# Summing the modulation rows over the partitions: from TensorE products with ones to DRAM transposes and GpSimd adds

## The chip, the cores and the metric

One core of a Trainium2 chip (trn2) runs the program once. The metric is the device time of that one execution in microseconds (us), lower is better. Times are given as the median of several runs of one build; the profile comes from one execution of its own.

## The reference, cut to what matters

The program computes two transformer-like blocks on 256 tokens of width 2048: a first block (a gated recurrence, dilated attention, output product) and a second block of two layers whose normalised inputs are modulated. Only the modulation is touched by the change:

```python
s_lat = jax.nn.silu(c)              # (1, 2048)
s_ctx = jax.nn.silu(c_ctx)          # (2048,)
for l in range(DEPTH_2):            # two layers
    shift, scale, gate = jnp.split((s_lat @ w_mod[l] + b_mod[l])[:, None, :], 3, axis=-1)
    shift_c, scale_c, gate_c = jnp.split(s_ctx @ w_mod[l] + b_mod[l], 3, axis=-1)
    hx = _rmsnorm(x, norm_g[l]) * (1.0 + scale) + shift
    hc = _rmsnorm(ctx, norm_g[l]) * (1.0 + scale_c) + shift_c
    ...
        ctx = ctx + gate_c * y_c
    x = x + gate * y
```

`w_mod[l]` is 2048 x 6144 in float32. A vector times this matrix is wanted for two vectors (one for the last gate).

## The kernel before

**The main work.** All large products run in *granules*: 256 rows of a weight matrix by 512 columns. ScalarE (ACT) writes the high half `w_hi` of the weights (line 607), VectorE (DVE) the low half `w_lo` (line 615), and TensorE (PE) does twelve products of 128x512 with them (lines 626, 627, 632). ACT and DVE may be up to four granules ahead (`NSPLIT = 4`). SyncE (SP) loads the weights into a ring of four slots (`raw`), each for two granules, in the order of the list `LOADS`. A granule `n` also carries side work, written out by hand at fixed numbers: attention, recurrence, normalisation. The stages are the first part (granules 0 to 223, four iterations of 56), the branches (`S2` on), the output product (`S3` on), and four streams of the second block, `c0`, `x0`, `c1`, `x1` (from `S4` on).

**The modulation.** `w_mod` is worked off in twelve *halves* (`HALVES`): a layer, a part (shift, scale or gate) and 1024 of its columns, for two vectors, or for one in halves 10 and 11. For each half, DVE multiplies 16 tiles of 128 rows by the vector's value of that row and adds them up into `rows` (128 partitions x 1024) for each vector, one operation at a time, at the granules that the table `HALVES` gives (`mod_row`, lines 2246 and 2250). What is left is the sum of `rows` over the 128 partitions.

Before, this sum is made by TensorE, in `mod_half` at the granules of the table `SUMS`: products with a column of ones into rows 0, 32, 64 and 96 of the PSUM tile `X[3]`.

```python
for j in range(2):
    for v in range(values):
        r = 32 * (values * j + v)
        last = pe.matmul(X[3][r:r + 1, :], ones, rows[h][v][:, CH * j:CH * (j + 1)], start=True, stop=True)
last.then_inc(mod_sums, 1)
```

Four granules later DVE copies the sums out of PSUM (`chunk_copy`, line 2259) or adds the gate's bias (`gate_add`, line 2267). GpSimd (POOL) sends shift and scale through DRAM (`col_mid`, line 794) so that they come back as columns over the partitions (`modcol`, line 797), to which DVE adds the bias (`columns_read`, line 2277); a gate goes to DRAM (`m_mid`, line 786), and is read from there over all partitions when a stream ends.

**Who else waits.** `mod_sums` also tells that the memory of `rows` is free. SP waits for it before two loads of the modulation's own slots (`load_own`, lines 546 and 561), ACT before it writes `o_hi`, `u_hi`, `m_hi`, `stg2` and `b_hi`, DVE before `u_lo` and before halves 4 and 7, and POOL before it loads half of the context `xr_p3` (line 924). This context is squared by ACT at granule `S3 + 13` (line 1500). POOL's program is a fixed order of its own: the first six halves, the two gates of layer 0, the loads around `S3`, then `windows`, `pairs` and `ends` of each stream. `windows` is a run of GpSimd adds and products (lines 856 to 867); `pairs(s)` gives the low half of two keys `kq_lo` (line 883) for each of four pairs of heads, which TensorE's scores (line 1302) take; in the first part `rope` on DVE (lines 2125 to 2132) turns queries and keys that TensorE then transposes (`t_qk`, line 961).

Of the kernel before, what the change touches and what calls it, by code (L numbers as in the profile page):

```python
# [15 lines left out]
F32 = mybir.dt.float32  # L16
F32R = mybir.dt.float32r
ALU = mybir.AluOpType
# [135 lines left out]
COLUMNS_BEFORE = [sum(not g for g in IS_GATE[:e]) for e in range(len(SUMS) + 1)]  # L154
GATES_BEFORE = [sum(IS_GATE[:e]) for e in range(len(SUMS) + 1)]
GATE_EVENTS = [e for e in range(len(SUMS)) if IS_GATE[e]]
LAYER_COLUMNS = [1 + max(COLUMNS_BEFORE[e] for e in range(len(SUMS)) if not IS_GATE[e] and HALVES[e].layer == l) for l in range(LAYERS)]

# [5 lines left out]
OPS_AT = [[(h, t, i) for g, h, t, i in OPS if g == n] for n in range(GRANULES)]  # L164

# [82 lines left out]
def build_program(nc, t, out):  # L248
    with ExitStack() as ctx:
# [63 lines left out]
        modchunk2 = at("modchunk2", rt + 36 * KB, [P, CH])  # L313
# [28 lines left out]
        gaterows = [at(f"gaterows{i}", a, [P, CH]) for i, a in enumerate((cm + 2048, cm + 2048, regU + 28 * KB, regH + 14 * KB))]  # L342
# [9 lines left out]
        ones = small[:, 40:41]  # L352
# [69 lines left out]
        col_mid = nc.dram_tensor("col_mid", (COLUMNS_BEFORE[-1], 2, HALF), F32, kind="Internal").ap()  # L422

# [46 lines left out]
        mod_chunk, mod_cols, mod_read = sem("mod_chunk"), sem("mod_cols"), sem("mod_read")  # L470
        mod_rows, mod_sums, rows_in = sem("mod_rows"), sem("mod_sums"), [sem(f"rows_in{i}") for i in range(2)]
# [60 lines left out]
        def load_own(sp, item):  # L532
# [8 lines left out]
            elif h == 9 and i == 4:  # L541

                sp.wait_ge(*ST[0].at("gpT_ps", 1))
                sp.wait_ge(*ST[0].at("win", 12))
            elif h == 7 and i == 3:
                sp.wait_ge(mod_sums, 7)
# [13 lines left out]
            elif h == 6:  # L560
                sp.wait_ge(mod_sums, 6)
# [75 lines left out]

        def chunk_of(e):

            return modchunk2 if e == 9 else modchunk  # L640
# [122 lines left out]
        def _(pool):  # L763

            pool.memset(modchunk[:, :], 0.0).then_inc(mod_zero, 1)
            pool.memset(ones, 1.0).then_inc(mod_zero, 1)
# [6 lines left out]
            def gate_bias(l, i, half, values):  # L773
                pool.memset(gaterows[i][:, :], 0.0).then_inc(mod_zero, 1)
                pool.wait_ge(mod_zero, 3 + i + 1)
                for j in range(2):
                    for v in range(values):
                        r, col = 32 * (values * j + v), HALF * half + CH * j
# [2126 lines left out]
```

## Time and profile before

| | |
|---|---|
| median of 3 runs | 2459.67 us (2459.33 to 2459.93) |
| the profiled execution's own time | 2459.43 us |
| its span in the trace | 2457.6 us |
| TensorE matmul busy | 2444.9 us, 99% |
| VectorE busy | 2079.3 us, 85% |
| ScalarE busy | 1279.9 us, 52% |
| GpSimd busy | 132.7 us, 5% |
| granted TensorE clock | 0.999 of full |
| DMA | 570.35 MB, 232 GB/s on the mean |

The span is what the trace covers; the execution's own time is 1.83 us longer. A busy TensorE means that matmul records follow each other without a gap; their ends are modelled, so the distance between two starts tells more than a record's length. In the rows, PE is TensorE's matmuls, DVE VectorE, ACT ScalarE, POOL GpSimd; "out<-in" names tiles by the program's names, and "idle before <-releaser" is how long the engine had nothing before the row, and what ended it.

### The profile page before, as it was taken

The page shows a single profiled execution, that of the slowest core. Times are in us where ns is not written, and L with a number is a line of the kernel's source. Part 1 is how long each engine was busy: PE and PEld are TensorE (multiplying, and loading weights), DVE is VectorE, ACT ScalarE, POOL GpSimd, SP SyncE. Part 2 cuts the span into 40 slices and gives each one's busy share as a digit, 9 for nine tenths or more (in the row PEclk, how much of TensorE's full clock was granted, in tenths as well). Part 3 has the DMA queues.
Part 4 walks back from the last instruction along what each step waited for, and adds up shares of the span by engine and source line. Part 5 has one row for each costly group of instructions (what it writes and reads, how often), then busy time and mean ns, then how long its engine had stood idle before and what let it go on. Part 6 is the DMA issues. An engine that isn't in the chain of part 4 may idle for free.

```text
span 2457.6 us, 30476 instructions
## 1 busy us (share of the span) xinstructions
PE 2444.9 (99%) x11640; PEld 2010.3 (82%) x11640; DVE 2079.3 (85%) x2655; ACT 1279.9 (52%) x1761; POOL 132.7 (5%) x196
## 2 busy tenths in 40 slices
PE   9999999999999999999999999999999999999998
PEld 7888888888788888888888888888888888888887
DVE  6999898898988998768999877898977885988876
ACT  6545544544554344454455654455565444456664
POOL 0000000000000000100200000110000000200000
PEclk9999999999999999999999999999999999999999
DMA  9877687586769787778655577754547876554464
GB/s 356 271 247 254 206 282 238 188 281 228 251 212 326 259 304 269 279 249 287 205 189 187 180 265 280 283 172 155 171 154 257 286 280 218 176 166 150 148 225 152
DMA packets 351905, 570.35 MB, mean 232 GB/s; under 512 B 19376, under 2 KB 204080, under 8 KB 347920
## 3 DMA queue, kind: packets, MB, share of 16 engines
q1 hardware_dynamic: 343232, 532.87, 63.7%
q0 software_dynamic: 7808, 34.79, 4.2%
q8 instruction: 92, 1.51, 0.3%
q10 hardware_dynamic: 720, 0.75, 0.1%
q14 instruction: 53, 0.43, 0.0%
HBM read 559.85 MB, written 8.48 MB: 231 GB/s over the span
## 4 chain that ended last, share of the span: by engine, by line
PE 97%; DVE 1%; issue 1%; ACT 0%; DMA 0%; SPq 0%; DVEq 0%
PE acc L626 30%; PE acc L627 29%; PE acc L632 29%; PE aux L961 3%; PE aux L1328 2%; PE aux L1302 1%; PE aux L1104 0%; PE aux L994 0%; DVE w_lo L615 0%; PE aux L1297 0%; DVE rows_u L2250 0%; PE aux L1051 0%; DMA raw<-in_w_in 0%; PE aux L1445 0%; PE aux L1443 0%
## 5 line engine op out<-in xcount | busy, mean ns | idle before, releaser
L607 ACT ACTIVATE w_hi<-raw 128x1024 fp32r<-128x1024 f32 x808 | 846.0, 1059 | 759.1 <-PE acc L632 643.0
L615 DVE TENSOR_TENSOR w_lo<-raw,w_hi 128x1024 fp32r<-128x1024 f32 x808 | 990.8, 1230 | 253.7 <-ACT w_hi L607 252.3
L626 PE MATMUL acc<-w_hi,h_hi 128*128 128x512 f32 x2240 | 885.6, 395 | 1.6 <-ACT w_hi L607 1.6
L627 PE MATMUL acc<-w_hi,h_lo 128*128 128x512 f32 x2240 | 873.1, 390 | 0.0
L632 PE MATMUL acc<-w_lo,h_hi 128*128 128x512 f32 x2240 | 600.6, 390 | 0.0
L626 PEld LDWEIGHTS acc<-w_hi,h_hi 128*128 128x128 f32 x2240 | 420.5, 188 | 96.5 <-issue 6.9
L632 PEld LDWEIGHTS acc<-w_lo,h_hi 128*128 128x128 f32 x2240 | 420.3, 188 | 89.5 <-DVE w_lo L615 0.7
L627 PEld LDWEIGHTS acc<-w_hi,h_lo 128*128 128x128 f32 x2240 | 420.7, 188 | 84.7
L626 PE MATMUL acc<-w_hi,u_hi 128*128 128x512 f32 x800 | 316.5, 396 | 0.0
L627 PE MATMUL acc<-w_hi,u_lo 128*128 128x512 f32 x800 | 312.0, 390 | 0.0
L632 PE MATMUL acc<-w_lo,u_hi 128*128 128x512 f32 x800 | 214.3, 390 | 0.0
L2599 DVE SCALAR_TENSOR_TENSOR cacc<-upad,wdw,cacc 128x256 f32<-128x256 f32 x360 | 192.6, 535 | 5.5
L626 PEld LDWEIGHTS acc<-w_hi,u_hi 128*128 128x128 f32 x800 | 150.2, 188 | 34.2 <-ACT w_hi L607 2.3
L632 PEld LDWEIGHTS acc<-w_lo,u_hi 128*128 128x128 f32 x800 | 150.2, 188 | 31.9
L627 PEld LDWEIGHTS acc<-w_hi,u_lo 128*128 128x128 f32 x800 | 150.2, 188 | 29.9
L2250 DVE SCALAR_TENSOR_TENSOR rows_u<-rows_in,smod,rows_u 128x1024 f32<-128x1024 f32 x75 | 97.8, 1311 | 0.1
L1798 ACT ACTIVATE prb<-aux,sm 128x512 f32<-128x512 f32 (+1 forms) x96 | 57.9, 616 | 37.8 <-DVE sm L2529 37.1
L2527 DVE TENSOR_REDUCE sm<-aux 128x1 f32<-128x512 f32 (+1 forms) x96 | 51.0, 595 | 3.7 <-PE aux L1302 3.6
L626 PE MATMUL acc<-w_hi,m_hi 128*128 128x512 f32 x128 | 50.7, 396 | 0.0
L627 PE MATMUL acc<-w_hi,m_lo 128*128 128x512 f32 x128 | 50.0, 390 | 0.0
L1806 ACT ACTIVATE aT<-aux 128x512 f32<-128x512 f32 (+1 forms) x48 | 22.6, 525 | 48.6 <-PE aux L1328 33.7
L794 POOL DMA_DIRECT2D col_mid<-modchunk x16 | 9.1, 568 | 717.9 <-DVE modchunk L2259 717.9
(389 smaller groups left out, 2165.7 us busy)
## 6 DMA issues: line engine op xcount, KB each, us to landing
raw<-in_w_in SPq DMA_DIRECT2D x630, 512.0 KB, 4.7
rows_in<-in_w_mod SPq DMA_DIRECT2D x120, 512.0 KB, 6.2
raw<-in_w_out SPq DMA_DIRECT2D x96, 512.0 KB, 4.8
raw<-in_w_mod SPq DMA_DIRECT2D x72, 512.0 KB, 5.7
raw<-in_w_rnn_out SPq DMA_DIRECT2D x32, 512.0 KB, 6.4
raw<-in_w_o SPq DMA_DIRECT2D x32, 512.0 KB, 8.0
raw<-in_w_attn_out SPq DMA_DIRECT2D x16, 512.0 KB, 4.9
xr_s<-x_mid POOLq DMA_DIRECT2D x4, 1024.0 KB, 12.2
```

Of the source, the lines that this page charges most:

```text
L607: act.activation(w_hi[:, n % NSPLIT], raw[:, slot, (n % 2) * SK:(n % 2) * SK + SK], ACT.Copy).then_inc(hi_ready, 1)
L615: dve.tensor_tensor(w_lo[:, n % NSPLIT], raw[:, slot, (n % 2) * SK:(n % 2) * SK + SK], w_hi[:, n % NSPLIT].bitcast(F32), ALU.subtract).the ...
L626: pe.matmul(acc[pair][m][:, :], a_hi[:, k0 + k, token(m)], w_hi[:, s, k], start=start and k == 0, stop=False)
L627: pe.matmul(acc[pair][m][:, :], a_lo[:, k0 + k, token(m)], w_hi[:, s, k], start=False, stop=False)
L632: last = pe.matmul(acc[pair][m][:, :], a_hi[:, k0 + k, token(m)], w_lo[:, s, k], start=False, stop=stop and k == SK - 1)
L961: return pe.transpose(dst.bitcast(F32R), src, ident[:, :])
L1302: last = pe.matmul(X[2 * comp + m][:, :], q_part[r, tokens], k_part[r, T:3 * T], start=i == 0, stop=i == 2)
L1328: last = pe.matmul(X[3][:, (2 * h + m) * P:(2 * h + m + 1) * P], aT[:, 4 * m + k], v, start=k == 0, stop=k == nk - 1)
L1798: act.activation(prb[:, b, 0:nk * P], X[b][:, 0:nk * P], ACT.Exp, bias=sm[:, 12 + b:13 + b], scale=SCALE2, accum_out=sm[:, 16 + b:17 + b]) ...
L2250: i = dve.scalar_tensor_tensor(out=dst, in0=src, scalar=smod[:, k, v:v + 1], in1=dst, op0=ALU.mult, op1=ALU.add)
L2527: step.link(dve.tensor_reduce(sm[:, 8 + b:9 + b], X[b][:, 0:nk * P], AX.X, ALU.max, negate=True))
L2599: i = dve.scalar_tensor_tensor(out=dst, in0=src, scalar=w, in1=dst, op0=ALU.mult, op1=ALU.add)
```

## The change

TensorE's products with ones, their copies out of PSUM and the semaphore `mod_sums` go. Each half is now summed by POOL alone. `rows_out` writes `rows` to DRAM (`row_mid`) in blocks of 128 columns. `fold` reads it back so that a partition holds 4 x 128 values of one column block, adds quarter on quarter, then halves; what is left (128 x 128) goes to DRAM again (`part_mid`) and is folded the same way on 16 (or 8) partitions. Then the bias is added and the result goes where it went before. Whoever waited for `mod_sums` now waits for `rows_gone`, the landing of the writes.

```diff
-SUMS = [(h, TAIL_SG[0] + 15 if h == 9 else AT[h][-1] + 2) for h in range(len(HALVES))]
+FOLDS = [[at(f"fold{i}{j}", off, [P, 4, P]) for j, off in enumerate(pair)] for i, pair in enumerate((
+    (regU + 12 * KB, regU + 14 * KB), (regO + 6 * KB, regO + 14 * KB), (cm + 2048, o3 + 28 * KB),
+    (rt + 6 * KB, rt + 101 * KB // 2)))]
+def rows_out(e):
+    pool.wait_ge(mod_rows, OPS_BEFORE[e + 1])
+    for v in range(HALVES[e].values):
+        pool.dma_start(row_mid[e][8 * v:8 * v + 8].rearrange("k p c -> p k c"),
+                       rows[e][v][:, :].rearrange("p (k c) -> p k c", k=8)).then_inc(rows_gone, 16)
+def fold(e, place):
+    x = HALVES[e]
+    a, b = FOLDS[place]
+    blocks = 8 * x.values
+    groups = P // blocks
...
+    def down(src, parts, count):
+        brought(pool.dma_start(a[0:parts], src[:, 0:4]))
+        for q in range(4, count, 4):
+            brought(pool.dma_start(b[0:parts], src[:, q:q + 4]))
+            pool.wait_ge(folding, folded)
+            added(pool.tensor_tensor(a[0:parts], a[0:parts], b[0:parts], ALU.add))
+        added(pool.tensor_tensor(a[0:parts, 0:2], a[0:parts, 0:2], a[0:parts, 2:4], ALU.add))
+        added(pool.tensor_tensor(a[0:parts, 0:1], a[0:parts, 0:1], a[0:parts, 1:2], ALU.add))
+    pool.wait_ge(rows_gone, GONE[e + 1])
+    down(row_mid[e][0:blocks].rearrange("k (g r) c -> (k g) r c", g=groups), P, P // groups)
+    brought(pool.dma_start(part_mid[e], a[:, 0]))
+    pool.wait_ge(folding, folded)
+    down(part_mid[e].rearrange("(k g) c -> k g c", g=groups), blocks, groups)
...
-for e in range(6):
-    move_columns(e)
+for e in range(3):
+    rows_out(e)
+    fold(e, 0)
+for e in (3, 4):
+    rows_out(e)
+    fold(e, 1)
+rows_out(5)
 pool.wait_ge(oT_lo, IT1)
...
+fold(5, 2)
+for e in (6, 7):
+    rows_out(e)
+    fold(e, 2)
...
                     for h in range(2):
                         pool.tensor_tensor(kq_lo[h][:, 2 * T:], kc[:, 2 * p + h, :], kq_hi[h][:, 2 * T:].bitcast(F32),
                                            ALU.subtract).then_inc(S["keys_r"], 1)
+                    if p < 2:
+                        fold((8, 9)[p] if s == 1 else (10, 11)[p], 3)
...
-            pool.wait_ge(mod_sums, 9)
+            rows_out(8)
+            pool.wait_ge(rows_gone, GONE[9])
             pool.dma_start(xr_p3[:, 0], t["ctx_2"][0][0:P, :]).then_inc(ST[0]["xr_in"], 16)
...
                         if it:

-                            act.wait_ge(mod_sums, U_FREE[it])
+                            act.wait_ge(rows_gone, GONE[U_FREE[it]])
```

Beside this, `windows` of `x0` and `x1` issues `rows_out(10)` and `rows_out(11)`, and `ends` of `c0` issues `rows_out(9)`. The last lines of the diff are one of the waits (ACT before `u_hi`); the others are changed in the same way, and half 4 on DVE and the last part of `o_hi` on ACT now wait for earlier folds to be done (`mod_read`).

The order of instructions shows three places. **TensorE at the end of the first iteration**, before (the sums of half 0):

```order
L632 MATMUL acc<-w_lo,h_hi 128x512 [waits lo_ready]
L632 MATMUL acc<-w_lo,h_hi 128x512 x3
L1104 MATMUL aux<-rows_u_117,small 1x512 [waits mod_rows]
L1104 MATMUL aux<-rows_u_118,small 1x512
L1104 MATMUL aux<-rows_u_117,small 1x512
L1104 MATMUL aux<-rows_u_118,small 1x512
L626 MATMUL acc<-w_hi,h_hi 128x512 [waits hi_ready,ev1_dve,ev1_act]
```

The four middle rows are gone, here and at the eleven other places (two rows for halves 10 and 11).

**POOL in stream x0**, between the key pieces of two pairs of heads, in the changed kernel; before, the third row here followed the second at once:

```order
L922 TENSOR_TENSOR kq_lo_186<-kc,kq_hi_184 128x256
L800 DMA fold_118<-row_mid 128x512 [waits rows_gone]
L802 DMA fold_119<-row_mid 128x512
L804 TENSOR_TENSOR fold_118<-fold_118,fold_119 128x512 [waits folding]
...
L806 TENSOR_TENSOR fold_118<-fold_118 16x128 [waits fold_step]
L826 DMA col_mid<-fold_118 16x128 [waits fold_step]
L831 DMA modcol_90<-col_mid 128x8x1 [waits folding]
L836 TENSOR_TENSOR modcol_90<-modcol_90,modbias 128x16 [waits folding]
L922 TENSOR_TENSOR kq_lo_185<-kc,kq_hi_183 128x256 [waits s_sc_ps,s_qkT_sb]
```

A whole fold (eight adds, one bias add, and ten loads and stores) now stands in front of the next pair's keys.

**POOL around the context load of `S3`**, before:

```order
L922 DMA xr_p_208<-in_ctx 128x2048 [waits m_lo_r,gate_out]
L924 DMA xr_p_208<-in_ctx 128x2048 [waits mod_sums]
L794 DMA col_mid<-modchunk 2x512 [waits mod_chunk]
```

and in the changed kernel:

```order
L960 DMA xr_p_211<-in_ctx 128x2048 [waits m_lo_r,gate_out]
L775 DMA row_mid<-rows_z_134 128x8x128 [waits mod_rows]
L775 DMA row_mid<-rows_z_135 128x8x128
L963 DMA xr_p_211<-in_ctx 128x2048 [waits rows_gone]
L860 DMA wdw<-in_columns 128x124
```

The second context load now waits for the landing of two stores that are issued behind the first one.

## Rows read from the trace of the kernel before

**Rows 1.** The page, chain that ended last: shares of the span.
```profile
PE 97%; DVE 1%; issue 1%; ACT 0%; DMA 0%; SPq 0%; DVEq 0%
```
**Rows 2.** Timeline of PE: start us, us, engine line op out<-in xcount.
```profile
169.49 1.07 PE L632 MATMUL acc<-w_lo,h_hi 128*128 128x512 f32 x4
170.48 1.04 PE L1104 MATMUL aux<-rows_u,small 128*1 128x512 f32 x8
...
171.79 0.39 PE L627 MATMUL acc<-w_hi,h_lo 128*128 128x512 f32 x1
...
173.41 1.07 PE L632 MATMUL acc<-w_lo,h_hi 128*128 128x512 f32 x4
...
174.54 0.39 PE L627 MATMUL acc<-w_hi,h_lo 128*128 128x512 f32 x1
```
**Rows 3.** Timeline of PE around the sums of half 11, of one vector.
```profile
2034.40 1.07 PE L632 MATMUL acc<-w_lo,u_hi 128*128 128x512 f32 x4
...
2036.69 0.39 PE L627 MATMUL acc<-w_hi,u_lo 128*128 128x512 f32 x1
```
**Rows 4.** Groups of POOL by shape: busy us, mean ns of one, idle before.
```profile
L858 POOL TENSOR_TENSOR win_a<-win_b 128x562 f32<-128x562 f32 x3 | 3.6, 1193 | 0.2
L864 POOL TENSOR_TENSOR win_b<-win_b,rcnt 128x256 f32<-128x256 f32 x6 | 5.6, 938 | 0.5
```
**Rows 5.** Timeline of DVE as POOL's adds of stream x0 begin.
```profile
1588.46 0.99 DVE L2599 SCALAR_TENSOR_TENSOR cacc<-upad,wdw,cacc 128x256 f32<-128x256 f32 x2
...
1590.52 4.08 DVE L2599 SCALAR_TENSOR_TENSOR cacc<-upad,wdw,cacc 128x256 f32<-128x256 f32 x2
1594.52 2.15 DVE L615 TENSOR_TENSOR w_lo<-raw,w_hi 128x1024 fp32r<-128x1024 f32 x1
```
**Rows 6.** Windows: us, PE PEld DVE ACT POOL busy, PEclk, DMA share, GB/s.
```profile
740.00:780.00 40.00, 40.00 (x193) 32.52 (x192) 35.66 (x36) 14.84 (x17) 5.62 (x10) 1.00 0.92 340
1590.00:1607.00 17.00, 17.00 (x77) 14.06 (x76) 16.86 (x14) 7.67 (x9) 15.44 (x14) 1.00 0.38 123
1640.00:1750.00 110.00, 110.00 (x566) 90.30 (x564) 97.89 (x164) 62.23 (x111) 4.31 (x6) 1.00 0.50 163
```
**Rows 7.** Tile view of `col_mid`: DMA issues to landing.
```profile
DMA to landing us min/median/max: 2.1/5.3/12.8
```
**Rows 8.** Timeline of DVE, two places.
```profile
326.65 0.28 DVE L2132 TENSOR_TENSOR qk<-qk,rtmp 128x128 f32<-128x128 f32 x1
...
772.13 1.23 DVE L615 TENSOR_TENSOR w_lo<-raw,w_hi 128x1024 fp32r<-128x1024 f32 x1
```
**Rows 9.** Timeline of PE, four places.
```profile
327.07 0.79 PE L961 MATMUL aux<-ident,qk_r 128*128 128x128 f32 x8
...
671.42 0.80 PE L961 MATMUL aux<-ident,qk_r 128*128 128x128 f32 x7 [1.22 <-DVE qk L2132]
...
774.54 1.07 PE L632 MATMUL acc<-w_lo,h_hi 128*128 128x512 f32 x4
...
1045.90 0.39 PE L626 MATMUL acc<-w_hi,m_hi 128*128 128x512 f32 x1
```
**Rows 10.** Groups of DVE by shape: what copies the sums out.
```profile
L2259 DVE COPY modchunk<-aux 128x512 f32<-128x512 f32 x8 | 5.5, 685 | 0.0
```
**Rows 11.** Timeline of POOL around `S3`.
```profile
1023.91 0.54 POOL L922 DMA_DIRECT2D xr_p<-in_ctx  x1 [82.97 <-DVE m_lo L2422]
1027.12 0.54 POOL L924 DMA_DIRECT2D xr_p<-in_ctx  x1 [2.67 <-PE aux L1104]
```
**Rows 12.** The page, DMA issues: xcount, KB each, median us to landing.
```profile
xr_p<-in_ctx POOLq DMA_DIRECT2D x2, 1024.0 KB, 8.5
```
**Rows 13.** Timeline of ACT at granules `S3 + 13` and `S3 + 14`.
```profile
1037.75 1.90 ACT L1500 ACTIVATE squares_out<-xr_p 128x2048 f32<-128x2048 f32 x1
...
1039.64 1.05 ACT L607 ACTIVATE w_hi<-raw 128x1024 fp32r<-128x1024 f32 x1
```
**Rows 14.** Waits of POOL: us in total, times, longest us.
```profile
POOL kq_lo L883 <- ACT kq_hi L1791: 311.3, 6, 51.9
```

More of the change, by code:

```diff
@@ L147 @@
 assert all(len(x.at) == 2 * x.values * HALF_TILES and x.at == sorted(x.at) for x in HALVES)
-SUMS = [(h, TAIL_SG[0] + 15 if h == 9 else AT[h][-1] + 2) for h in range(len(HALVES))]
 IS_GATE = [x.part == 2 for x in HALVES]
[L154 to L157, printed above, removed]
+COLUMNS_BEFORE = [sum(not g for g in IS_GATE[:e]) for e in range(len(HALVES) + 1)]
+GATES_OUT = [16 * sum(HALVES[i].values for i in range(e + 1) if IS_GATE[i]) for e in range(len(HALVES))]
+LAYER_COLUMNS = [1 + max(COLUMNS_BEFORE[e] for e in range(len(HALVES)) if not IS_GATE[e] and HALVES[e].layer == l) for l in range(LAYERS)]
 OPS_BEFORE = [0]
@@ L164 @@
 OPS_AT = [[(h, t, i) for g, h, t, i in OPS if g == n] for n in range(GRANULES)]
+GONE = [0]
+for x in HALVES:
+    GONE.append(GONE[-1] + 16 * x.values)
 def rows_after(h, t):
@@ L769, in _ @@
             pool.tensor_copy(ident[:, :], ident_in[:, :]).then_inc(const_in, 1)
[L773 to L778, printed above, removed]
-                        pool.dma_start(gaterows[i][r:r + 1, :], t["b_mod_2"][l:l + 1, 2 * D + col:2 * D + col + CH]).then_inc(tables_in, 16)
@@ L781, in gate_rows @@
-            def gate_rows(l, i, half, values):
-                pool.wait_ge(mod_chunk, GATE_EVENTS[i] + 1)
-                for j in range(2):
-                    for v in range(values):
-                        r, col = 32 * (values * j + v), HALF * half + CH * j
-                        pool.dma_start(m_mid[l, v:v + 1, col:col + CH], gaterows[i][r:r + 1, :]).then_inc(gate_out, 16)
-            def move_columns(e):
-                c = COLUMNS_BEFORE[e]
-                l, first = HALVES[e].layer, HALVES[e].part * KT + 8 * HALVES[e].half
-                pool.wait_ge(mod_chunk, e + 1)
-                for j in range(2):
-                    pool.dma_start(col_mid[c][:, CH * j:CH * (j + 1)], chunk_of(e)[64 * j:64 * j + 33:32, :]).then_inc(mod_cols, 16)
-                pool.wait_ge(mod_cols, 64 * c + 32)
-                for v in range(2):
-                    pool.dma_start(modcol[l][:, first:first + 8, v], col_mid[c][v].rearrange("(k p) -> p k", p=P),
-                                   allow_slow_non_contiguous=True).then_inc(mod_cols, 16)
@@ L1704, in sides @@
                         if chunk:
-                            act.wait_ge(mod_sums, (0, 6, 8, 8)[chunk])
+                            act.wait_ge(rows_gone, GONE[(0, 6, 8, 8)[chunk]])
                             if chunk != 2:
```

160 lines of the change are left out of this document (60 added, 100 removed).

## The prediction

> **What bounds the kernel now.** I began with the chain of waits that ended last: 97% of the span is TensorE [rows 1], and the product lines 626, 627 and 632 hold nearly all of it. So whatever leaves TensorE's queue shortens the run by its full spacing, as long as its helpers keep their lead: ACT and DVE prepare each granule, and TensorE stalls only where that preparation comes late. I then read the timelines of PE, DVE, ACT and POOL side by side, to see how far ahead the preparation is, and looked for the few places where it is nearly late. The question of this change is how much of a sure gain on TensorE is given back there. The clock plays no part: the windows show it at 1.00, the upper level of 2.4 GHz, and TensorE has no pause in which that would change [rows 6].
>
> **What is removed.** From the first `w_lo` product of a granule to the second product of the next one takes 174.54 - 173.41 = 1.13 us; with the sums between them 171.79 - 169.49 = 2.30 us [rows 2]. One half costs 1.17 us. The sums of half 11, of one vector and half as many products, take just as much: 2036.69 - 2034.40 = 2.29 us [rows 3], so the number of products does not count here. Twelve halves: 12 x 1.17 = **14.0 us off TensorE**. They all lie on the chain, so they count in full. DVE loses twelve copies or adds of about 0.69 us [rows 10] and eight small bias adds; POOL loses its few memsets and its small DMAs. None of these is on the chain.
>
> **What is added on POOL.** A half costs two stores of 512 KB (one for halves 10 and 11), then a fold: seven transfers one after the other (three quarters of `row_mid`, the first two loads side by side; `part_mid` out; `part_mid` in; `col_mid` or the bias; `modcol` or `m_mid`), and nine adds. A POOL add takes 1.19 us for 562 elements and 0.94 for 256 [rows 4]. So four adds of 512 at about 1.12, two of 256 at 0.8 to 0.9, two of 128 at about 0.6 and a small bias add make some 7.6 us. A transfer: those of `col_mid` land after 5.3 us in the median, 2.1 at best and 12.8 at worst [rows 7]. A fold is thus 7 x 5.3 + 7.6 = about 45 us, with 22 and 97 as the bounds if every transfer were the best or the worst. Two halves are about 100 us apart, so POOL itself has time. What this does to others is the point.
>
> **DVE beside POOL's adds.** While POOL is busy 15.4 of 17 us [rows 6], DVE's operations stretch: a pair of taps from 0.99 to 4.08 us, `w_lo` from 1.23 to 2.15 [rows 5]. These two pieces are the first of eight in that stretch; the six after them lose 0.5 to 0.9 us each, and all eight 8.1 us: about 0.5 us of DVE for each us of POOL. The bounds are none (DVE was waiting anyway) and 1. Where DVE's lead is several us this is covered. In the first part it is not covered everywhere: the transposes of rotated queries and keys start at 327.07, and DVE's last piece for them ends at 326.65 + 0.28 = 326.93; those at 671.42 even waited 1.22 us for DVE [rows 8, 9]. There DVE is one granule ahead, not four. Half 1 ends at about 269 and its fold runs from about 278 to 325; half 4 ends at 622.5 and its fold runs from about 632 to 680. DVE works without a gap from about 309 to 327 and from about 651 to 671. Into the first stretch fall the small adds of the fold's second half, some 2.5 us: 1.3 us of DVE, less the 0.14 of slack and a little that DVE no longer does: +1.0. Into the second fall one add of 512, the two small ones, and the three of the second half, 5 us: +2.4. Sum **+3.4 us**, bounds 0 and 7.
>
> **SBUF ports.** In the stretch above, POOL's adds cost DVE about half their time. The Trainium skill (SBUF — State Buffer, Who interferes with whom) speaks against this change: a DVE instruction with two SBUF inputs and a GpSimd instruction that reads SBUF use one shared interface, and the one that comes second blocks for the whole of the other. By that rule each us of POOL would cost DVE up to a full us; the first pair of taps looks like it, the stretch as a whole does not.
>
> **DMA near 770 us.** From 740 to 780 us the DMA engines are busy 0.92 of the time at 340 GB/s [rows 6], and this is where the weights arrive last: `w_lo` is ready at 772.13 + 1.23 = 773.36, and TensorE takes it at 774.54 [rows 8, 9], a lead of 1.18 us. The first loads of fold 5 fall here, together 1 MB: at 340 GB/s 3.1 us of transfer more, and 1 us of adds beside DVE, less the copy of 0.6 to 0.7 at this place that goes [rows 10]: late by 3.4, stall **+2.2 us**. If the loads spread over a longer time it is 0; if SP also waits for the stores of half 5 before its own loads behind them, 6.
>
> **The context at `S3`.** Before, the two context loads are issued at 1023.91 and 1027.12 and land after 8.5 us each, the second at 1035.6 [rows 11, 12]. ACT squares it at 1037.75, and the next `w_hi`, ready at 1039.64 + 1.05 = 1040.7, is wanted by TensorE at 1045.90 [rows 13, 9]. So the second load may come 2.1 + 5.2 = 7.3 us later without a stall. In the change, two stores are issued behind the first load, at about 1024.5, and take the place of the second load: they land at about 1035.8. Then the second load is issued and needs its 8.5 us: 1044.3, late by 8.7, stall **+1.4 us**. Bounds: 0 if it lands in 6 us or so, 6 if the stores take 5 us longer.
>
> **Other waits** I take at nothing. `u_hi` and `u_lo` of iterations 1 to 3 come more than 10 us after the stores of the half before have landed; `m_hi` of the third branch chunk comes 17 us after half 7's last row; halves 9 to 11 leave behind waits that stood there before. If the cover were gone each would cost ACT a few us. The DMA engines carry 2 x 10 + 1 x 2 = 22 MB more on 570, mostly where they have room.
>
> **Sum**, against the profiled execution: 2459.43 - 14.0 + 3.4 + 2.2 + 1.4 = 2452.4. The median stands 0.24 above that execution: **2452.7 us**. About 0.2% (4.9 us) is what a measurement of this kernel can tell from no change; 7.0 us is over it.
>
> **The rivals.** *All is covered.* If DVE's losses fall into its idle time and the transfers into gaps, only the 14.0 us remain: 2445.7. For it: DVE is busy 85% on the whole. Against it: the three places above, where the lead is 0.1, 1.2 and 7 us.
>
> *Full blocking.* If each us of POOL costs DVE a full us, the places cost 2.3, 4.9 and (3.1 + 2 - 0.6 - 1.2) = 3.3, with the context's 1.4 together 11.9: 2457.6, no change. The first pair of taps, 3.1 us lost in 4, speaks for it; 8.1 lost in 15.4 over the whole stretch, against it. It is the rule of the SBUF page named above.
>
> *The folds hold up the keys (slower).* In streams `x0` and `x1` folds 8 to 11 stand between the key pieces of two pairs of heads. POOL waited 51.9 us there for ACT [rows 14]; with the 1.7 us until TensorE's scores begin a fold may last 53.6. At 45 us it fits. But all seven transfers are in series, and one that is late moves TensorE, which has nothing else to do then. Each of four folds costs its excess: with folds of 60 us 4 x 6.4 = 25.6, so 2478.3; it outweighs the gain of 7.0 from 55.4 us on. For it: the landing times up to 12.8. Against it: from 1640 to 1750 us the DMA engines are busy only 0.50 at 163 GB/s [rows 6], while the median of 5.3 comes mostly from busier stretches. The Trainium skill (DMA: Bandwidth & Descriptors, Anatomy of one DMA) gives about 2.0 us fixed and bytes at 436 GB/s for a transfer; by that a fold is an estimated 24 us and this rival falls away.
>
> *Late stores.* If a store of a half takes 15 us and more, SP, ACT at `u_hi` and the context all wait: 5 to 10 us more each, 2460 to 2475.
>
> **How the numbers follow.** My forecast's mechanism (2449.5 to 2456.5) 0.45, all covered 0.22, full blocking 0.19, the keys 0.09, late stores 0.05. Below 2454.8 lie the second, and most of the first: faster 0.59. Within 0.2%, up to 2464.6: the rest of the first, full blocking, half of late stores: 0.29. Slower 0.12. The range leaves out some of the bottom, where 2445.7 is nearly a floor, and the keys: 2446.0 to 2463.5; the bounds of the three stalls together (0 and 19, less 14.0) would reach from 2445.7 to 2464.7.
>
> **What would show it.** In the changed profile granules without side work should follow each other at 2.72 us at the former twelve places, with no L1104. POOL's busy time should grow by about 90 us to 220. Rows of DVE beside POOL's adds should be longer by half of these. PE should wait at the transposes near 320 and 660 for DVE, and stand near 765 and near 1035 on `w_hi` or `w_lo`. A fold should last about 45 us from its first load to its last, and the key pieces in `x0` and `x1` should still wait for ACT. I am wrong in my main step if TensorE's gaps sum to less than 3 or more than 11 us; if `kq_lo` is released by a fold, the keys' rival has it; if TensorE stands on `squares_out` for over 5 us, the stores were priced too low.

## The result and the profile after

The changed kernel takes **2486.88 us** (median of 4 runs, 2486.24 to 2487.21), the kernel before 2459.57 us (2459.33 to 2459.93) beside it: ratio 1.011, 95% interval 1.0097 to 1.0122. It is 27.3 us slower; the forecast was 7.0 us faster, with a range up to 2463.5. The profiled execution took 2487.15 us, with a span of 2485.3.

The page of the changed kernel, with what answers to the table of before and to [rows 1]: busy times (us, share, instructions), then the chain that ended last.

```profile
PE 2445.2 (98%) x11552; PEld 2015.3 (81%) x11552; DVE 2122.4 (85%) x2635; ACT 1275.9 (51%) x1761; POOL 344.8 (14%) x385
...
PE 72%; DVE 14%; DMA 5%; issue 5%; ACT 3%; SPq 0%; POOL 0%; DVEq 0%; ACTq 0%; POOLq 0%
```

TensorE held 97% of the chain before; now DVE, the DMA queues and ACT stand in it with 22%. POOL grew by 212 us (forecast: 90): 158 of them are the adds of the folds, the rest is mostly the issuing of transfers, which the page counts as busy. DVE grew by 43 although it lost twelve copies.

The saving itself is there. The timeline of PE where the first sums were, which answers to [rows 2]:

```profile
172.34 1.07 PE L635 MATMUL acc<-w_lo,h_hi 128*128 128x512 f32 x4
...
175.06 1.07 PE L635 MATMUL acc<-w_lo,h_hi 128*128 128x512 f32 x4
```

2.72 us from granule to granule, where 3.92 stood. Set side by side product by product, the two timelines of PE show this step of 1.1 to 1.2 us at eleven of the twelve places. At the twelfth (half 9, 1431 us before) only 0.4 us are gained, because a wait of 0.47 us for `w_hi` takes the sums' place. So 13.3 us left TensorE, for the 14.0 of the forecast. What ate them, the waits of PE (us in total, times, longest):

```profile
PE aux L995 <- DVE qk L2133: 10.1, 5, 4.9
PE acc L629 <- ACT w_hi L610: 8.2, 6, 4.8
PE aux L995 <- DVE og L2155: 7.7, 2, 4.7
PE acc L635 <- DVE w_lo L618: 1.8, 4, 0.7
PE aux L995 <- DVE prb L2504: 1.7, 1, 1.7
PE aux L1150 <- POOL rx L765: 1.3, 1, 1.3
PE aux L1309 <- DVE u_lo L2528: 0.6, 1, 0.6
PE aux L1085 <- DVE xc L2176: 0.3, 1, 0.3
```

That is 31.7 us, against 4.5 in the kernel before (qk 1.6, `w_hi` 1.6, `rx` 1.3). 27.2 of waits do not make up 27.7 + 13.3 = 41.0. The next part is the clock. The windows of 8 us right behind four of the waits (columns as in [rows 6]):

```profile
568.98:576.98 8.00, 8.00 (x34) 6.69 (x35) 8.00 (x8) 3.26 (x5) 2.05 (x3) 0.79 0.68 205
686.79:694.79 8.00, 8.00 (x29) 6.62 (x30) 6.53 (x6) 2.88 (x4) 0.90 (x1) 0.65 0.76 257
1069.00:1077.00 8.00, 8.00 (x24) 6.40 (x25) 5.36 (x8) 7.23 (x8) 0.00 (x0) 0.65 0.88 283
2258.12:2266.12 8.00, 8.00 (x36) 6.65 (x36) 7.93 (x10) 4.53 (x6) 5.18 (x5) 0.79 0.42 134
```

PE is busy all of the time, with a granted clock of 0.65 to 0.79 on the mean: part of each window ran at the lower level of 1.2 GHz (from 686 to 692 us the windows show 0.50 throughout). 8 x (0.21 + 0.35 + 0.35 + 0.21) = 9.0 us lost behind the waits, not in them. In the timeline a product stands 0.43 us from the next there and not 0.23. So 36 of the 41 us have a name; the rest is in steps too small for a row of their own. The kernel before shows 1.00 in the 8 us behind its longest inner wait, 1.22 us at 671.42 [rows 9].

By place, from the two timelines of PE (waits with the clock behind them, at times of the kernel before): fold 0 at 218 us 3.0; fold 1 at 307 and 328 4.1; fold 3 at 561 6.4; fold 4 from 650 to 675 9.0; fold 5 near 780 some 2; the context at 1046 7.8; fold 11 at 2233 4.0; small steps elsewhere together some 5. These are the places where a fold runs beside; how much of each the fold itself causes is taken apart behind the experiments.

What the adds of a fold took (POOL by shape: busy us, mean ns of one, idle before):

```profile
L804 POOL TENSOR_TENSOR fold<-fold,fold 128x512 f32<-128x512 f32 x32 | 58.5, 1828 | 156.2 <-DMA fold<-row_mid 156.2
L804 POOL TENSOR_TENSOR fold<-fold,fold 16x512 f32<-16x512 f32 x10 | 20.7, 2066 | 42.8 <-DMA fold<-part_mid 42.8
...
L806 POOL TENSOR_TENSOR fold<-fold 16x128 f32<-16x128 f32 x10 | 11.8, 1181 | 0.8
```

1.83 us for 512 elements on the mean (forecast 1.12), and a small add on 16 partitions costs as much as one on 128: 2.07 us for 512 elements and 1.18 for 128 (forecast for the last: about 0.6). These means hold the waits for DVE. The adds that met none took 1.28, 0.80 and 0.53 us for 512, 256 and 128 elements, on 128 partitions and on 16, close to the forecast. A fold took 48 to 60 us from its first load to its last add in the first eight, 43 in `x0` and 29 in `x1`, for the forecast's 45.

### The profile page after: what moved, and what is told of

It reads as the page before. It is cut to its first block, busy times and chain, and to the rows that moved or that the text cites. A ratio compares the mean times of both kernels' runs of the same rounds, so it can differ in the third digit from the quotient of the medians.

```text
span 2485.3 us, 30445 instructions
## 1 busy us (share of the span) xinstructions
PE 2445.2 (98%) x11552; PEld 2015.3 (81%) x11552; DVE 2122.4 (85%) x2635; ACT 1275.9 (51%) x1761; POOL 344.8 (14%) x385
## 4 chain that ended last, share of the span: by engine, by line
PE 72%; DVE 14%; DMA 5%; issue 5%; ACT 3%; SPq 0%; POOL 0%; DVEq 0%; ACTq 0%; POOLq 0%
PE acc L629 22%; PE acc L630 22%; PE acc L635 22%; DVE w_lo L618 5%; DMA raw<-in_w_in 3%; PE aux L995 2%; ACT w_hi L610 1%; PE aux L1335 1%; DVE rows_m L2251 1%; DVE rows_u L2251 1%; PE aux L1309 1%; DVE rows_o L2251 1%; DMA rows_in<-in_w_mod 1%; DMA raw<-in_w_mod 1%; DVE cacc L2561 0%
## 5 line engine op out<-in xcount | busy, mean ns | idle before, releaser
L618 DVE TENSOR_TENSOR w_lo<-raw,w_hi 128x1024 fp32r<-128x1024 f32 x808 | 1001.4, 1244 | 250.8 <-ACT w_hi L610 249.2
L2561 DVE SCALAR_TENSOR_TENSOR cacc<-upad,wdw,cacc 128x256 f32<-128x256 f32 x360 | 201.2, 559 | 5.5
L804 POOL TENSOR_TENSOR fold<-fold,fold 128x512 f32<-128x512 f32 (+2 forms) x48 | 89.3, 1861 | 210.8 <-DMA fold<-row_mid 156.2
```

The lines of the kernel that those rows point to most:

```text
L618: dve.tensor_tensor(w_lo[:, n % NSPLIT], raw[:, slot, (n % 2) * SK:(n % 2) * SK + SK], w_hi[:, n % NSPLIT].bitcast(F32), ALU.subtract).the ...
L804: added(pool.tensor_tensor(a[0:parts], a[0:parts], b[0:parts], ALU.add))
L2561: i = dve.scalar_tensor_tensor(out=dst, in0=src, scalar=w, in1=dst, op0=ALU.mult, op1=ALU.add)
```

## The experiments

The theory to start from: POOL's adds slow DVE, DVE's lead is thin in the first part, and TensorE waits. The rival: the folds' loads and stores do it. Thirteen kernels answer; times are medians of 4 to 10 runs, which lie within 0.3 to 5.5 us of each other, each group beside its own runs of the kernel before (2459.42 to 2459.62).

**1. The adds left out.** In `down`:

```diff
-                        added(pool.tensor_tensor(a[0:parts], a[0:parts], b[0:parts], ALU.add))
-                    added(pool.tensor_tensor(a[0:parts, 0:2], a[0:parts, 0:2], a[0:parts, 2:4], ALU.add))
-                    added(pool.tensor_tensor(a[0:parts, 0:1], a[0:parts, 0:1], a[0:parts, 1:2], ALU.add))
+                    pool.wait_ge(folding, folded)
```

> All nine of POOL's adds inside a fold are left out but the last bias add of shift and scale, so the modulation is not summed; every store, load and wait of POOL stays. In the changed kernel's trace TensorE loses about 41 us in stalls against the 14 it gains: some 33 at places beside a fold, 7.6 at the context. Theory A (the adds slow DVE, which has little lead there): these 33 go, the context stays: 2486.9 - 32 = about 2455, between 2452 and 2458. Theory B (the folds' loads and stores delay the weights): no more than 5 us of it goes: 2482 to 2487. Theory C (half and half): near 2470.

(The gate's bias add stays as well: the eight adds of `down` are what is left out.)

Measured: 2463.99 us (ratio 1.0017, 1.0008 to 1.0026), between theory A's range and theory C. The adds cost 22.9 us and are the largest part, but not the 32 that theory A gave them.

**2. The folds' loads left out as well.** Both `down` calls and the store of partial sums are replaced by one memset.

```diff
-                down(row_mid[e][0:blocks].rearrange("k (g r) c -> (k g) r c", g=groups), P, P // groups)
-                brought(pool.dma_start(part_mid[e], a[:, 0]))
-                pool.wait_ge(folding, folded)
-                down(part_mid[e].rearrange("(k g) c -> k g c", g=groups), blocks, groups)
+                added(pool.memset(a[0:blocks, 0:1], 0.5))
```

> The fold's loads, its store of partial sums, their loads and all adds are left out too (the modulation is not summed); a memset of 16 values takes their place. The stores of rows to DRAM and everything that waits for them stay, and so do the last small transfers. Theory A: as without adds, within 1.5 us: 2453 to 2456. Theory B: this is where the time goes, 2452 to 2455 and at least 20 us under the kernel without adds. The context's 7.6 us stay in both.

Measured: 2457.07 us, above both ranges. The folds' loads, without any adds, cost 6.9 us; both theories had this wrong, A by calling it nothing.

**3. Tiny stores.**

```diff
-                    pool.dma_start(row_mid[e][8 * v:8 * v + 8].rearrange("k p c -> p k c"),
-                                   rows[e][v][:, :].rearrange("p (k c) -> p k c", k=8)).then_inc(rows_gone, 16)
+                    pool.dma_start(row_mid[e][8 * v, 0:1, :], rows[e][v][0:1, 0:P]).then_inc(rows_gone, 16)
```

> As the kernel without folds, but each store of rows is one partition's 512 bytes, so the stores' bytes go too, while the order of waits stays (the modulation is not summed). Both theories: the context's stall falls from 7.6 us to under 2, and about 2446 to 2449 remains, which is the kernel before less 12 x 1.17. If it stays at 2453 the context's stall is not the stores' length but the order of POOL's queue.

Measured: 2451.5 us (ratio 0.9966, 0.9955 to 0.9978). The context's stall went from 5.6 to 0.4 us, so it was the stores' length. But the time is above the expected range, and 6 us above the 2445.4 that TensorE's queue alone would give, with next to nothing left of the change. Two waits for DVE remain: 1.1 us at 557 and 3.45 at 669, with the clock at 0.79 in the 8 us behind that one. The windows view of this kernel:

```profile
640.00:680.00 40.00, 36.55 (x166) 29.96 (x165) 37.00 (x42) 15.07 (x18) 0.00 (x0) 0.96 0.63 212
```

DVE is busy 37.0 of 40 us, and POOL not at all. By 632 us TensorE had gained 5 x 1.1 us, DVE had not, and here they meet. (That DVE's load is the cause is an argument up to here; experiment 9 tests it.)

**4. The order at the context.**

```diff
+            rows_out(8)
             pool.wait_ge(m_lo_r, 2 * NCH)
             pool.dma_start(xr_p3[:, 1], t["ctx_2"][0][P:2 * P, :]).then_inc(ST[0]["xr_in"], 16)
-            rows_out(8)
             pool.wait_ge(rows_gone, GONE[9])
```

> Only the order at the context: the two stores of half 8 are issued before POOL waits for the last low half of the third branch, ahead of the first context load instead of behind it. Half 8 is ready about 5 us before that wait ends. If the 7.6 us there are the stores' landing, they shrink to under 2: 2486.9 - 6 = about 2481, between 2479 and 2483. If the stall has another origin (the DMA engines are full, and the load itself is late), under 2 us go: 2485 to 2487.

The place in the changed kernel, POOL and then PE, which answers to [rows 9, 11]:

```profile
1044.35 0.57 POOL L960 DMA_DIRECT2D xr_p<-in_ctx  x1 [42.14 <-DVE m_lo L2384]
1044.90 1.83 POOL L775 DMA_DIRECT2D row_mid<-rows_z  x2
1057.27 0.56 POOL L963 DMA_DIRECT2D xr_p<-in_ctx  x1 [10.53 <-DMA row_mid<-rows_z]
```
```profile
1069.00 0.80 PE L629 MATMUL acc<-w_hi,m_hi 128*128 128x512 f32 x1 [4.84 <-ACT w_hi L610]
```

Measured: 2486.74 us (2485.23 to 2490.47): no change that can be told from none, as the second case has it. The edit did what it should: the second context load is issued 7.4 us behind the first and no longer 12.9. But TensorE then waits in two places (timeline of PE, this kernel):

```profile
1054.94 0.50 PE L629 MATMUL acc<-w_hi,m_hi 128*128 128x512 f32 x1 [2.07 <-ACT w_hi L610]
...
1068.93 0.50 PE L629 MATMUL acc<-w_hi,m_hi 128*128 128x512 f32 x1 [2.55 <-ACT w_hi L610]
```

Before the first of them ACT waited 5.85 us for `raw<-in_w_o`, before the second 4.42, while its square no longer waits for the context (7.03 us in the changed kernel). So the late transfer is now one of the weights and not the context. That the stores and the context's loads, now closer together, delay the weights is the likely reading; no run here tests it by itself.

**5. The adds made twice.** Each of the three lines of experiment 1 stands twice in a row.

> Each of a fold's adds but the bias adds is made twice (the modulation's values are changed by it), with the same loads, stores and waits. In the changed kernel the adds keep POOL busy 158 us and, against the kernel without them, cost 22.9 us of time. Theory A (POOL and DVE slow each other while both work): the second helping costs at least as much as the first, since the cover is used up: 2486.9 + 23 to 45 = 2510 to 2532, with more and longer waits of TensorE for DVE. Theory B (a fold that ends later holds up those who wait for it): TensorE, ACT or DVE would be released by POOL, and 13 us more per fold would cost nothing where a fold ends 50 us early: 2487 to 2495.

Measured: 2533.2 us (ratio 1.0299), 46.3 us more, a little over the range of theory A. The second helping costs twice the first. Theory B is out: no wait of TensorE names a fold; those for DVE (`qk`, `prb`, `og`, `w_lo`, `xc`) rose from 21.6 to 49.2 us.

**6. Only the adds on 128 partitions.**

```diff
-                        added(pool.tensor_tensor(a[0:parts], a[0:parts], b[0:parts], ALU.add))
+                        if parts == P:
+                            added(pool.tensor_tensor(a[0:parts], a[0:parts], b[0:parts], ALU.add))
+                    if parts < P:
+                        pool.wait_ge(folding, folded)
+                        return
```

> Of the adds only the five on 128 partitions stay in each fold (for two vectors); the adds on 16 or 8 partitions are left out, so the modulation is not summed. The small ones are about a third of POOL's add time (some 50 of 158 us). Theory A1 (what counts is how long POOL works, however few partitions): a third of the 22.9 us goes: 2476 to 2481. Theory A2 (an add on 16 partitions hardly disturbs DVE): 2485 to 2488.

Measured: 2475.24 us (2473.27 to 2476.65), 0.8 below A1's range and far from A2's. Half of the 22.9 us belongs to the adds on 16 or 8 partitions, which do some 6% of the arithmetic of the others (896 x 16 beside 1920 x 128 elements). They are 60 of the 148 us of the adds left out in experiment 1, 40% and not the third that was expected. A2 is out: few partitions are no cheaper.

**7. Half 5's work moved behind the transposes, with tiny stores and no folds**, by the table of halves.

```diff
     Half(1, 0, 1, 2, None, tiles_at((3 * SG1, (
-        45, 46, 46, 47, 48, 48, 49, 50, 53, 53, 54, 55)), (S2, (
-        0, 0, 1, 4, 5, 5, 6, 7, 10, 10, 11, 12, 13, 17, 17, 18, 18, 19, 19, 20)))),
+        52, 52, 53, 53, 54, 54, 55, 55)), (S2, (
+        0, 0, 1, 2, 3, 4, 5, 5, 6, 7, 8, 9, 10, 11, 12, 13, 14, 15, 16, 17, 18, 19, 19, 20)))),
```

> The kernel with tiny stores and no folds (the modulation is not summed; 2451.5 us, with 3.45 us of TensorE waiting for DVE at the transposes near 669 us and a lower clock behind it), and the multiply-adds of half 5 that stood in the seven granules ahead of that place are moved behind it by the table of halves, with the same work in all. Theory (DVE sets the pace there, so TensorE's gain of the four halves before is lost at it): the wait goes and the clock stays up: 2451.5 - 5 = about 2446.5, between 2445 and 2448. Rival (the weights come late, DVE only passes it on): 2450 to 2452.

Measured: 2455.22 us, worse by 3.7 and outside both ranges. The wait at 669 is gone (5.1 us less there, with the clock), but 7.1 us came back behind it, with waits of 1.26 us at 717 and this one, in the timeline of PE:

```profile
733.27 0.94 PE L991 MATMUL aux<-ident,s_sb_r 128*128 128x128 f32 x9 [3.29 <-DVE og L2151]
```

From 680 to 735 us DVE is now busy 48.3 of 55 us and was 45.3 in experiment 3's kernel: the room behind the transposes is as small as the room ahead of them.

**8. The same move in the changed kernel.**

> The changed kernel with the same move of half 5's multiply-adds and nothing else. Theory: the 9.0 us that TensorE loses around 672 us go, with a part coming back at the transposes after it because fold 4 still runs: 2478 to 2482. Rival (DVE is behind everywhere there and the loss only moves): 2484 to 2488.

Measured: 2488.65 us, 0.65 above the rival's range, and the rival's case: in the timelines of PE 8.2 us go between 640 and 700 us, and 9.4 come between 700 and 760.

**9. Less work for DVE, with tiny stores and no folds.** It tests the same theory as 7 without moving work to another place where DVE has no room.

```diff
                 dst = rows[h][v][:, :].rearrange("p (a c) -> p a c", a=2)
+                if 3 <= h <= 5 and (tile or j):
+                    src, dst = src[:, 0:1, :], dst[:, 0:1, :]
```

> The kernel with tiny stores and no folds (the modulation is not summed; 2451.5 us), and in halves 3 to 5 each of DVE's multiply-adds but the first of a half works on 512 of its 1024 columns (0.7 in place of 1.3 us), with the same loads. Theory (DVE's own load is what keeps TensorE from taking its whole gain between 540 and 780 us): no wait for DVE is left there, also not the 1.22 us of the kernel before: 2451.5 - 5.3 = about 2446, between 2445 and 2448. Rival (weights that land late, whatever DVE does): 2450 to 2453.

Measured: 2445.57 us (ratio 0.9944, 0.9929 to 0.9959). With room on DVE TensorE takes its whole gain. The window that answers to experiment 3's:

```profile
640.00:680.00 40.00, 40.00 (x192) 33.39 (x191) 32.44 (x42) 17.04 (x19) 0.00 (x0) 1.00 0.79 274
```

DVE 32.4 in place of 37.0 us, TensorE without a gap, and 0.79 of the DMA engines' time in place of 0.63: the weights were not what was late. Beside experiment 3's kernel 1.3 us are gained at 557 and 5.3 around 669, and nothing over 0.3 elsewhere.

**10. The same in the changed kernel.**

> The changed kernel, whole folds, with the same smaller multiply-adds in halves 3 to 5 (part of the modulation is not computed). TensorE loses 16 us there between 560 and 680 us. Theory (a fold costs only what DVE's lead does not cover): under 4 us of it stay and the rest of the run is as it was: 2471 to 2477. Rival (a fold costs TensorE the same whether DVE has time or not): 2483 to 2487.

Measured: 2472.17 us (2469.30 to 2473.95), 14.7 less. Of the 16 us between 560 and 680 a wait of 2.3 stays (in the profiled execution, the fastest of the four). A fold costs what DVE cannot cover.

**11. The folds' adds without the loads between them.** `down` loses its loads and their waits, and `a` and `b` are set to zero first.

> The folds' adds in full, on zeros, without the folds' loads and without the store of partial sums (the modulation is not summed); the stores of rows stay. Without its loads a fold's adds follow each other at once, some 13 us in one piece. The kernel without loads and adds takes 2457.1 us, loads without adds cost 6.9, loads and adds 29.8. Theory (adds and loads cost apart): 2457.1 + 22.9 = 2480, between 2475 and 2485. Rival (the adds hurt because they come in single pieces over 50 us and wait for DMA in between): under 2470, if one compact stretch fits into DVE's lead.

Measured: 2488.72 us, 31.7 above the kernel without folds and outside both ranges: one compact piece is no better, and adds and loads do not add up. The adds cost 31.7 us without the loads and 22.9 beside them; adds and loads together cost 29.8. So the split between them depends on the order in which they are taken away. (The 24 memsets that this kernel adds are free, by experiment 13.) This kernel also shows how an add acts. POOL, then DVE in this kernel, then DVE at the same place in the kernel of experiment 9, where POOL is idle:

```profile
173.75 4.16 POOL L801 TENSOR_TENSOR fold<-fold,fold 128x512 f32<-128x512 f32 x3
```
```profile
172.97 0.74 DVE L2166 TENSOR_SCALAR qk<-acc,small 128x512 f32<-128x512 f32 x1
173.85 1.47 DVE L2123 TENSOR_TENSOR rtmp<-qk,rope 128x256 f32<-128x256 f32 x1
175.36 1.40 DVE L2125 TENSOR_TENSOR qk<-qk,rope 128x256 f32<-128x256 f32 x1
176.86 1.20 DVE L2129 TENSOR_TENSOR qk<-qk,rtmp 128x128 f32<-128x128 f32 x1
```
```profile
173.87 0.42 DVE L2122 TENSOR_TENSOR rtmp<-qk,rope 128x256 f32<-128x256 f32 x1
174.33 0.42 DVE L2124 TENSOR_TENSOR qk<-qk,rope 128x256 f32<-128x256 f32 x1
174.86 0.29 DVE L2128 TENSOR_TENSOR qk<-qk,rtmp 128x128 f32<-128x128 f32 x1
```

Three adds of 1.39 us, and three DVE operations of 0.42, 0.42 and 0.29 us that each last about as long as an add: DVE lost 2.9 us in 4.2. `L2166`, ahead of them, stands beside a memset of POOL and keeps its time. It also works the other way. Two adds of the changed kernel (POOL, then DVE, fold 0):

```profile
187.36 4.14 POOL L804 TENSOR_TENSOR fold<-fold,fold 128x512 f32<-128x512 f32 x1 [5.38 <-DMA fold<-row_mid]
...
198.34 1.29 POOL L804 TENSOR_TENSOR fold<-fold,fold 128x512 f32<-128x512 f32 x1 [5.99 <-DMA fold<-row_mid]
```
```profile
186.80 1.27 DVE L2251 SCALAR_TENSOR_TENSOR rows_b<-rows_in,smod,rows_b 128x1024 f32<-128x1024 f32 x1
188.00 2.34 DVE L618 TENSOR_TENSOR w_lo<-raw,w_hi 128x1024 fp32r<-128x1024 f32 x2
190.27 1.00 DVE L2138 SCALAR_TENSOR_TENSOR s_sb<-aux,mask 128x384 f32<-128x384 f32 x2
...
198.46 2.25 DVE L618 TENSOR_TENSOR w_lo<-raw,w_hi 128x1024 fp32r<-128x1024 f32 x1 [2.09 <-ACT w_hi L610]
```

The first add begins while DVE works. The three operations with two inputs in SBUF keep their times, and the add ends 1.16 us after the last of them: POOL paid 2.9 us, DVE nothing. The second begins 0.12 us ahead of `w_lo`. It keeps its time, and `w_lo` takes 2.25 us in place of 1.22: DVE pays. So who pays is settled by who comes first, and a us of POOL's adds cost DVE less than a us on the mean. Not every operation of DVE takes part. These two rows of the changed kernel (DVE, then POOL) overlap, and both have the times that they have alone:

```profile
1694.11 2.48 DVE L2489 TENSOR_REDUCE sm<-aux 128x1 f32<-128x512 f32 x4 [0.24 <-PE aux L1309]
```
```profile
1695.90 1.28 POOL L804 TENSOR_TENSOR fold<-fold,fold 16x512 f32<-16x512 f32 x1 [4.12 <-DMA fold<-part_mid]
```

`aux` is in PSUM; DVE's other operations with an input in PSUM keep their times beside adds as well.

**12. Copies in place of adds.**

```diff
-                        added(pool.tensor_tensor(a[0:parts], a[0:parts], b[0:parts], ALU.add))
+                        added(pool.tensor_copy(a[0:parts], b[0:parts]))
```

(and the two lines after it in the same way)

> Each add of a fold but the bias adds becomes a POOL copy of the same shape, one input in place of two (the modulation is not summed); loads, stores and waits stay. Theory A (DVE loses while POOL reads SBUF, in proportion to POOL's time): the cost over the kernel without adds falls with POOL's busy time; copies of about half the adds' duration would give 2464.0 + 11 = 2475, between 2468 and 2481. Theory B (it is the number of instructions, each holding up one DVE operation for good, whatever its length): 2484 to 2488. Theory C (only two-input instructions of POOL disturb DVE): 2462 to 2466.

Measured: 2468.71 us, 4.7 over the kernel without adds. It lies at the lower end of A's range, but A's proportion does not hold: the copies keep POOL busy for 94 us and the adds for 148, which would give 14.6. B is out, since there are as many instructions. C nearly fits: a copy costs something, but far less than an add.

**13. Memsets in place of adds**, `pool.memset(a[0:parts], 0.0)` and so on.

> As the copies, with memsets of the same shape: POOL only writes (the modulation is not summed). A memset of 128x512 took 0.53 us in the kernel with adds alone. Theory A1 (it is POOL's reading that DVE waits for): nothing but the loads and stores is left, 2462 to 2466, and DVE's small operations beside the memsets keep their 0.4 and 0.3 us. Theory A2 (any use of SBUF by POOL counts, in proportion to its time): 100 memsets of 0.5 us are a third of the adds' time: about 2464 + 7 = 2471, between 2468 and 2474.

Measured: 2462.89 us, as without adds (2463.99): A1. 38 of DVE's `w_lo` lie beside a memset and take 1.22 us, the time that they take alone; 60 lie beside a fold's add in the changed kernel and take 1.45 on the mean, up to 2.31. The small operations of `rope` beside a memset keep their 0.4 us. By shape, POOL of experiments 12 and 13:

```profile
L804 POOL COPY fold<-fold 128x512 f32<-128x512 f32 x32 | 37.3, 1165 | 156.4 <-DMA fold<-row_mid 156.4
```
```profile
L804 POOL MEMSET fold<- 128x512 f32 x32 | 17.0, 530 | 154.4 <-DMA fold<-row_mid 154.4
```

**DVE's loss against the end time.** DVE's busy time on each page, less that of the same kernel without the adds (2072.8 us with the loads, 2071.9 without):

| POOL's work in the folds | DVE busy | DVE's loss | end time | share that reaches the end |
|---|---|---|---|---|
| memsets | 2071.5 | -1.3 | -1.1 | - |
| copies | 2086.5 | 13.7 | 4.7 | 0.34 |
| adds on 128 partitions | 2102.4 | 29.6 | 11.3 | 0.38 |
| all adds | 2122.4 | 49.6 | 22.9 | 0.46 |
| all adds, no loads | 2123.9 | 52.0 | 31.7 | 0.61 |
| all adds twice | 2173.8 | 101.0 | 69.2 | 0.69 |

With the loads in place, the share that is not covered grows with DVE's loss. In the kernel without loads the adds stand in one piece, and a larger share of about the same loss reaches the end.

**The bill.** 2459.6 less 14.0 (products with ones) is 2445.6; DVE as the pace-maker in the first part +5.9 (2451.5); the stores +5.6 (2457.1); the folds' loads +6.9 (2464.0); the adds +22.9 (2486.9), in this order of taking them away. Experiment 9 comes out at 2445.57, but it is no exact measurement of the first term: the sums give 13.3 us, its lighter DVE also takes away the wait of 1.22 us that the kernel before had at 671, and small waits for `w_hi` stand against that.

The same bill by place, from the timelines of PE of the profiled executions, set side by side product by product (us; times of the kernel before; the sums' own gain of 13.3 left out):

| place | in all | DVE's pace | stores | loads | adds |
|---|---|---|---|---|---|
| fold 0, 218 | 3.0 | 0 | 0 | 0 | 3.0 |
| fold 1, 307 and 328 | 4.1 | 0 | 0 | 0 | 4.0 |
| fold 3, 561 | 6.4 | 1.3 | 1.0 | 2.2 | 2.0 |
| fold 4, 650 to 675 | 9.0 | 3.9 | 0 | 1.3 | 3.9 |
| the context, 1046 | 7.8 | 0.7 | 4.9 | 0.6 | 1.6 |
| fold 11, 2233 | 4.0 | 0 | 0 | 0 | 4.0 |
| elsewhere | 6.8 | 0.4 | 0.4 | 0.5 | 5.4 |

DVE's pace is experiment 3's kernel against the kernel before, the stores are 2 against 3, the loads 1 against 2, the adds the changed kernel against 1. Each is one execution, so a sum differs from the medians' by up to 2.3 us. Only a quarter of the adds' cost lies at 561 and 671; there the pace and the loads cost more than the adds. And the loads cost time at places where TensorE waits for DVE (561, 671), not only near 770; why DVE is later there with the loads is open.

Even with adds that cost DVE nothing (experiment 13) the layout through DRAM ends at 2462.9, above the kernel before.

## Why the prediction was wrong, step by step

- **Products off TensorE, 14.0 us.** The size was nearly right (13.3: half 9 gave 0.4 and not 1.17). "They all lie on the chain, so they count in full" failed: between 540 and 680 us DVE sets the pace, and 5.9 us of the gain are lost there before the stores and folds cost anything (experiments 3 and 9). The sign was in [rows 9]: TensorE's wait of 1.22 us for DVE says that TensorE is already as early there as DVE lets it be.
- **DVE beside POOL's adds, 3.4 us (bounds 0 and 7).** This is the step that failed most: 22.9 us. What DVE loses in all would have come out nearly right, but by luck: 0.5 us of DVE per us of POOL, on the 91 us of adds that the forecast's durations give, is 45 us, and 49.6 were measured. In fact the adds took 148 us and cost DVE a third of that; the two errors cancel. What was mis-sized is the cover. I counted only what falls into the last gapless stretch ahead of the transposes near 327 (+1.0, the adds cost 4.0 with the wait at 307) and 671 (+2.4, the adds cost 3.9 of the 9.0 us there), and took the lead elsewhere as enough: that is where the other 16 us of the adds are. But a DVE that is busy 0.93 of the time (experiment 3) does not make up a loss within a granule or two, so what a fold takes from DVE (49.6 / 12 = 4.1 us on the mean) arrives at the next wait. The outputs at 218 and 561 and the probabilities at 2233 were not looked at: the adds cost 3.0, 2.0 and 4.0 there.
- **The adds' durations.** 158 us and not 91. The forecast's 1.12, 0.8 to 0.9 and 0.6 us are close to what undisturbed adds took (1.28, 0.80, 0.53), on few partitions too; these would make about 99 us, an estimate from the shortest rows. The other 60 are POOL's waits for DVE, for which the forecast had no term: it let only DVE pay.
- **The clock.** "It plays no part" held only for the kernel before. Behind three waits of 4.7 to 4.9 us and one of 1.7 it fell to the lower level for a part of the next 8 us: 9.0 us of loss, for which the sum had no term.
- **DMA near 770 us, +2.2.** Some 2 in the timelines: size and place were right, the cause in part. With tiny stores and no folds nothing is lost there; the stores add 0.8, the loads 0.5, and the adds the rest.
- **The context, +1.4.** TensorE waited 4.84 us there, and the clock behind it cost 2.8 more. The mechanism was right (experiment 3: 4.9 of the 7.8 us go with the stores' bytes), the size was not, and the order of POOL's queue alone is not it: with the order changed the weights are late instead (experiment 4). The stores landed 1.0 us later than forecast (12.9 us from the first load's issue to the second's, for 11.9), and the load waited 2.2 us longer relative to TensorE (19.8 us from the first load's issue to the time when TensorE wants `w_hi`, for 22.0), since DVE's `m_lo`, which releases it, was late too. 1.4 + 1.0 + 2.2 = 4.6, without the clock.
- **"Other waits at nothing"**: the folds' loads cost 6.9 us in the kernel without adds, of which the timeline shows about 0.5 us near 770, the only place where I had put them, and 3.5 at 561 and 671, where DVE's lead is thin.
- **The rivals.** *All is covered* fell with its cover. *Full blocking* was right about a single instruction of DVE that comes second, and wrong about the mean (a third of a us per us of POOL, since POOL often comes second and pays itself) and about the sum (2457.6), for the same reason as my own: it, too, was counted at three places only. The Trainium skill (SBUF — State Buffer, Who interferes with whom) has the rule that the one that comes second waits for the whole of the other if DVE has two SBUF inputs and GpSimd reads SBUF. The traces bear it out: 0.42 us that became 1.47, the add that waited for three operations of DVE, reductions from PSUM that kept their 0.68 beside an add, and memsets that cost nothing. The keys' rival did not come true: `kq_lo` still waited up to 51.9 us for ACT, as in [rows 14]. *Late stores* did not come true as stated, though the size at the context (7.8 us) is within its 5 to 10: no transfer of `row_mid` took more than 11.2 us, for its 15.
- **What would show it.** My own limit was a sum of TensorE's gaps over 11 us; it is 27. The granules at 2.72 us, the waits for DVE at the two transposes and the keys' release by ACT came as forecast; the folds' 45 us came roughly (43 to 60, and 29 in `x1`).

## What to carry to other kernels

An instruction taken off the bounding engine is worth its time only as far as the next wait of that engine for another one that has no room: look for the waits that exist already. In this kernel, work for GpSimd that reads SBUF was paid for by VectorE, at up to a whole GpSimd instruction for each operation with two inputs in SBUF, whatever the number of partitions; the loss must be summed over the whole stretch in which VectorE has no gaps. And a wait of TensorE of over 3.3 us is priced too low by its own length: in all cases but one here the clock behind it cost another 1.5 to 3.2 us.

## What the runs showed of the hardware

- An add of POOL on 16 partitions took as long as on 128: 2.07 and 1.83 us on the mean for 512 elements, 1.18 and 1.17 for 128; undisturbed 1.28 for 512 and some 0.53 for 128 on either.
- An add of POOL and an operation of DVE with two inputs in SBUF did not run side by side, and the one that came second waited: an add of 1.28 us took up to 4.14, a DVE operation of 0.42 us up to 1.50. Reductions and operations with an input in PSUM kept their times (0.68 us beside an add and alone). A small `sm<-sm` of DVE, from SBUF to SBUF with one input, did not: 0.17 us alone, 0.59 and 0.66 beside an add.
- POOL's memsets of 512 elements stayed at 0.53 us and cost DVE nothing; its copies, 0.61 us undisturbed, came to 1.17 on the mean and cost DVE 13.7 us in all.
- Behind TensorE's waits of over 3.3 us the granted clock was 0.60 to 0.81 on the mean over the next 8 us in 30 of the 31 cases of all traces, and 1.00 in the other (3.41 us, experiment 5, at 457). After waits of 1.0 to 1.2 us it was 0.99 or 1.00 in 14 of 15. Between these the runs differ: waits of 2.8 to 3.1 us at the same place, 219 us, left it at 1.00 in three traces and gave 0.79 in three; 1.67 us at 2258, with other short waits close to it, gave 0.79, and 1.66 and 1.74 at the same place in two other traces 1.00.
